# Modulation vectors on VectorE during the first projection, pool sums on GpSimd: one layer block on one core

## What is computed

```python
mod_x = silu(c) @ w_mod + b_mod                  # [1024] @ [1024, 6144]
mod_c = silu(c_ctx) @ w_mod + b_mod
sh1, sc1, gt1, sh2, sc2, gt2 = split(mod_x, 6)   # csh1, csc1 from mod_c

h_x = rmsnorm(x, g_pre_mix) * (1 + sc1) + sh1    # h_c likewise from ctx
u, q, k, v = split(h_x @ w_in, 4)                # k and v also of h_c
attn = neighbourhood_attention(q, k, v, k_c, v_c, rpb)
pool = pool_mixer(u)       # 4 groups: windowed means of 2, 4, 8, 16 tokens minus u, @ pool_w
x = x + gt1 * rmsnorm(concat(pool, attn) @ w_out, g_post_mix)
h = rmsnorm(x, g_pre_mlp) * (1 + sc2) + sh2
x = x + gt2 * rmsnorm(square(relu(h @ w_mlp_in)) @ w_mlp_out, g_post_mlp)
```

## Time and profile before

| | us |
|---|---|
| median of 3 runs | 858.69 |
| lowest, highest | 855.11, 858.84 |
| the profiled execution, its own time | 856.64 |
| its span in the trace | 854.8 |
| u, q (from the first whole blocks) | 36 to 57 |
| k and v, with products 16 to 23 | 57.2 to 109.6 |
| near attention, to the last product with V | 109.7 to 152.1 |

### The profile page before, as it was taken

How to read it: one execution, slowest core, us unless ns; L and a number is a source line. 1 busy time by engine, 2 the same in 40 slices (tenths; PEclk the granted TensorE clock), 3 DMA queues, 4 the chain that set the end, 5 groups by cost and what they waited for, 6 DMA issues and landing times.

```text
span 854.8 us, 12416 instructions
## 1 busy us (share of the span) xinstructions
PE 826.4 (97%) x4602; PEld 674.8 (79%) x4602; DVE 546.7 (64%) x956; ACT 462.3 (54%) x873; POOL 44.8 (5%) x55
## 2 busy tenths in 40 slices
PE   5899999989999999999999999999999999999996
PEld 2697855868888888878888888887666788888885
DVE  2363278668887767557666666587566576666653
ACT  4573256466546545556555555566766565555542
POOL 1010000000000000000000000049000000000000
PEclk9999999999999999999999999999999999999999
DMA  9975549517987765247666655185023376666501
GB/s 349 373 315 208 204 157 355 178 47 238 323 274 248 226 199 176 91 142 275 206 210 202 198 188 163 38 335 181 26 78 120 99 256 219 215 202 213 176 1 50
DMA packets 45099, 165.76 MB, mean 194 GB/s; under 512 B 4976, under 2 KB 5104, under 8 KB 44784
## 3 DMA queue, kind: packets, MB, share of 16 engines
q1 hardware_dynamic: 44752, 164.45, 56.6%
q10 hardware_dynamic: 288, 0.52, 0.2%
HBM read 163.91 MB, written 1.05 MB: 193 GB/s over the span
## 4 chain that ended last, share of the span: by engine, by line
PE 75%; issue 1%; DVE 1%; ACT 1%; POOLq 0%; POOL 0%; ACTq 0%; DVEq 0%
PE ps L1465 23%; PE ps L1467 12%; PE ps L1492 11%; PE ps L1494 11%; PE ps L1496 11%; PE ps L1701 1%; PE ps L1775 1%; PE ps L1726 1%; PE ps L1745 1%; PE ps L1703 0%; PE ps L1938 0%; DVE sc L1135 0%; PE ps L1485 0%; PE ps L1487 0%; PE ps L1486 0%
## 5 line engine op out<-in xcount | busy, mean ns | idle before, releaser
L944 DVE TENSOR_TENSOR lo<-raw,hi 128x1024 fp32r<-128x1024 f32 (+2 forms) x247 | 294.0, 1218 | 119.1 <-ACT hi L502 118.8
L1465 PE MATMUL ps<-T,hi 128*128 128x512 f32 x864 | 303.7, 392 | 0.0
L502 ACT ACTIVATE hi<-raw 128x1024 fp32r<-128x1024 f32 (+2 forms) x247 | 249.6, 1044 | 14.7 <-DMA raw<-in_w_in_k 6.1
L1467 PE MATMUL ps<-T,lo 128*128 128x256 f32 x864 | 243.7, 282 | 0.0
L1465 PEld LDWEIGHTS ps<-T,hi 128*128 128x128 f32 x864 | 162.2, 188 | 35.0
L1492 PE MATMUL ps<-hi,T 128*128 128x512 f32 (+2 forms) x504 | 169.9, 395 | 0.7 <-DVE T L1215 0.7
L1494 PE MATMUL ps<-lo,T 128*128 128x512 f32 (+2 forms) x504 | 167.0, 389 | 0.0
L1496 PE MATMUL ps<-hi,T 128*128 128x512 f32 (+2 forms) x504 | 166.8, 389 | 0.0
L1467 PEld LDWEIGHTS ps<-T,lo 128*128 128x128 f32 x864 | 163.4, 189 | 2.4
L1496 PEld LDWEIGHTS ps<-hi,T 128*128 128x128 f32 x504 | 94.6, 188 | 19.8
L1494 PEld LDWEIGHTS ps<-lo,T 128*128 128x128 f32 x504 | 94.7, 188 | 19.4
(11 more groups left out here) (212 smaller groups left out, 759.2 us busy)
## 6 DMA issues: line engine op xcount, KB each, us to landing
raw<-in_ffn_down SPq DMA_DIRECT2D x44, 512.0 KB, 3.6
raw<-in_w_mod_p SPq DMA_DIRECT2D x40, 512.0 KB, 6.0
raw<-in_ffn_gate SPq DMA_DIRECT2D x40, 512.0 KB, 4.4
raw<-in_ffn_up SPq DMA_DIRECT2D x40, 512.0 KB, 4.2
raw<-in_w_mlp_out SPq DMA_DIRECT2D x32, 512.0 KB, 4.5
raw<-in_w_mlp_in SPq DMA_DIRECT2D x28, 512.0 KB, 4.5
raw<-in_w_out SPq DMA_DIRECT2D x16, 512.0 KB, 5.2
raw<-in_w_in_q SPq DMA_DIRECT2D x8, 512.0 KB, 5.7
```

What stands on the lines that cost most here:

```text
L502: e.activation(HI[SLOT[h]][:, 0:w], raw[n % RAW][:, 0:w], ACT.Copy).then_inc(s_hi, 1)
L944: e.tensor_tensor(LO[SLOT[h]][:, 0:w], raw[n % RAW][:, 0:w], HI[SLOT[h]][:, 0:w], ALU.subtract).then_inc(s_lo, 1)
L1465: e.matmul(o, a[:, k * P:(k + 1) * P], X[:, k].rearrange("p s w -> p (s w)"), start=(k == 0), stop=(k == KT - 1), skip_group_check=True)
L1467: m = e.matmul(o[:, 0:L], b[:, k * P:(k + 1) * P], Xh[:, k, :], start=False, stop=(k == KT - 1), skip_group_check=True)
```

## The change

It rearranges how sh2, sc2 and gt1 are made, and what goes along with it:

- sh2 and sc2: their part of w_mod is stored turned (`w_mod_c`, 16 chunks of kind "T", 128 output columns each, all 1024 inputs along the row). The vector c is spread over all partitions by one more transfer (into `G2`, which is free until the MLP), ScalarE applies silu to it (128x1024), and VectorE takes a dot product per chunk, `tensor_tensor_reduce` with the sum going straight into a column of `sh2` or `sc2`.
- gt1: eight more chunks of `w_mod_r`, summed by VectorE into `acc` as gt2 is.
- The order of the stream puts all 24 chunks between w_in_k 0 and w_out 2. They are worked off in `split` of VectorE, in the order of the stream. TensorE's products 16 to 39, `mod_turned` and `mod_part` are gone.
- `window(g)` moves word for word from VectorE to GpSimd, behind the clearing of its buffer.
- ScalarE makes all four copies of V, and both turned tiles of each near-attention step.
- Chunks 0 to 2 of w_out are split before the near attention, 3, 4 and 5 in its iterations 1, 3 and 8. ScalarE splits w_in_k 1 to 3 between its copies of q.
- The transfer of the gt2 bias into `G2` is issued later (at chunk H[40]), after a wait on both additions of the sh2 and sc2 biases.

```diff
     s = []
     for j in range(4):
         s += u[j:j + 1] + c[4 * j:4 * j + 4]
-    s += q + k[0:2] + c[16:18] + k[2:3] + c[18:21] + k[3:4] + c[21:24] + v + c[24:30]
-    for j in range(4):
-        s += o[j:j + 1] + c[30 + 3 * j:33 + 3 * j]
-    s += o[4:]
+    s += q + k[0:1] + d[0:1] + k[1:2] + d[1:3] + k[2:3] + d[3:6] + k[3:4] + d[6:9] + v[0:1] + d[9:12] + v[1:2] + d[12:]
+    s += v[2:3] + m[0:3] + v[3:4] + o[0:1] + m[3:5] + o[1:2] + m[5:8] + o[2:]
...
+        W_OUT_SPLIT = {1: 3, 3: 4, 8: 5}
...
# SyncE
                 if n == CH_AT["w_in_q", 0]:
+                    e.dma_start(silr, row[5:6, :].partition_broadcast(P)).then_inc(s_row, 16)
# GpSimd, behind the memset of pw
+            for g in range(4):
+                window(g)
# ScalarE
+            e.wait_ge(s_row, 16)
+            e.activation(silr, silr, ACT.Silu).then_inc(s_silr, 1)
             for a in range(4):
                 h = CH["w_in_q", a]
+                if a:
+                    split(CH["w_in_k", a])
...
-            mod_part(0)
             split(CH["w_in_v", 3])
             load_table(ACT.Exp)
+            split(CH["w_out", 2])
...
-            for i in (0, 2):
+            for i in range(4):
                 e.activation(V[:, i, :], ps[i][:, :], ACT.Copy).then_inc(s_vv, 1)
...
-                        e.wait_ge(s_ntr, 2 * m + 1)
...
-                        e.activation(PT1[2 * m % 4], ps[2][:, :], ACT.Copy).then_inc(s_npa, 1)
-                    if n in (3, 7):
-                        mod_part(n // 3)
-                    if 3 <= n < 9:
-                        split(CH["w_out", n - 3])
+                        for hh in range(2):
+                            e.wait_ge(s_ntr, 2 * m + hh + 1)
+                            e.activation(PT1[(2 * m + hh) % 4], ps[2 + hh][:, :], ACT.Copy).then_inc(s_npt, 1)
+                    if n in W_OUT_SPLIT:
+                        split(CH["w_out", W_OUT_SPLIT[n]])
# VectorE, sum_mod
+                if name == "w_mod_c":
+                    at = (sh2, sc2)[j // 8][:, j % 8:j % 8 + 1]
+                    e.wait_ge(s_silr, 1)
+                    e.tensor_tensor_reduce(out=r, in0=r, in1=silr, scale=1.0, scalar=0.0, op0=ALU.mult, op1=ALU.add,
+                                           accum_out=at).then_inc(s_msum, 1)
+                    return
...
# VectorE, behind the splits of w_in_u
-            split(CH["w_in_k", 2])
-            for g in range(3):
-                window(g)
-            split(CH["w_in_k", 3])
-            window(3)
-            split(CH["w_in_v", 1])
-            mod_part(0)
-            split(CH["w_in_v", 3])
+            split(CH["w_out", 2])
+            for v, dst in enumerate((sh2, sc2)):
+                e.wait_ge(s_msum, 8 * v + 8)
+                e.tensor_tensor(dst, dst, col(("b_sh2", "b_sc2")[v]), ALU.add).then_inc(s_mcol, 1)
...
-            for i in (1, 3):
-                e.tensor_copy(V[:, i, :], ps[i][:, :]).then_inc(s_vv, 1)
...
-                        e.tensor_copy(PT1[(2 * m + 1) % 4], ps[3][:, :]).then_inc(s_npd, 1)
-                    if n in (3, 7):
-                        mod_part(n // 3)
-                    if 3 <= n < 9:
-                        split(CH["w_out", n - 3])
+                    if n in W_OUT_SPLIT:
+                        split(CH["w_out", W_OUT_SPLIT[n]])
# TensorE
                 wstat(CH["w_in_k", a], ROT[a], 2)
-                for n in range(*((16, 16), (16, 18), (18, 21), (21, 24))[a]):
-                    mod_product(n)
...
-                if j == 1:
-                    e.wait_ge(s_k, 2)
-                    e.wait_ge(s_const, 1)
-                    mod_turned(0, 4)
...
-                        mod_product(24 + 2 * n)
-                        mod_product(25 + 2 * n)
...
-                    if n == 5:
-                        mod_turned(1, 7)
```

More of the change, by code:

```diff
@@ L55, in stream_plan @@
 def stream_plan():
-    c = [("w_mod_p", j, 1024, "C") for j in range(40)]
+    c = [("w_mod_p", j, 1024, "C") for j in range(16)]
+    m = [("w_mod_r", j, 1024, "M") for j in range(16)]
+    d = [("w_mod_c", j, 1024, "T") for j in range(16)]
     u, q, k, v = ([("w_in_" + name, j, 1024, "H") for j in range(4)] for name in "uqkv")
@@ L428, in _, with window @@
             e.memset(big[:, 8960:8960 + 4 * UP], 0.0).then_inc(s_pwz, 1)
+            def window(g):
+                before, n = uT[:, g, :], (WIN[g - 1] if g else 0)
+                e.wait_ge(s_u, g + 1)
+                e.wait_ge(s_pwz, 1)
+                for s in range(g + 1):
+                    a0, a1 = (1, 0) if s == 0 else (1 << (s - 1), 1 << (s - 1))
+                    e0, e1 = (a0 if s == 0 else a0 + 1), UP - a1
+                    if s:
+                        e.wait_ge(s_win, n)
+                    e.tensor_tensor(pw[s][:, e0:e1], before[:, e0 - a0:e1 - a0], before[:, e0 + a1:e1 + a1],
+                                    ALU.add).then_inc(s_win, 1)
+                    before, n = pw[s], n + 1
+                e.wait_ge(s_win, n)
+                e.wait_ge(s_inv, 16)
+                e.tensor_tensor(dT[:, g, :], before[:, 8:8 + L], inv[:, g, :], ALU.mult).then_inc(s_win, 1)
+                e.wait_ge(s_win, n + 1)
+                e.tensor_tensor(dT[:, g, :], dT[:, g, :], uT[:, g, 8:8 + L], ALU.subtract).then_inc(s_win, 1)
+            for g in range(4):
+                window(g)
             def scales(b):
@@ L1528, in quarter_turned @@
                                  stop=True)
-                m.then_inc(s_rowT, 1)
-            def mod_turned(v, bank):
-                e.wait_ge(s_rowA, v + 5)
-                e.wait_ge(s_rowD, v + 1)
-                for j in range(KT):
-                    m = e.matmul(ps[bank][:, j:j + 1], acc[:, j * P:(j + 1) * P], ones[:, 0:1], start=True, stop=True)
                 m.then_inc(s_rowT, 1)
```

143 lines of the change are left out of this document (40 added, 103 removed).

## The result

The changed kernel takes 854.72 us (median of 20 runs, 852.23 to 858.05) where the kernel before takes 860.07 on the same chip (20 runs): a ratio of 0.994 (0.9922 to 0.9957), or 5.3 us less. The forecast was 847.5, with 853.5 as its upper end. So the change is a gain, of about half the size forecast. The interval stays clear of no change, but 0.6% is little above the 0.5% that I had named as the least that such a measurement tells.

The account below looks back on a forecast made before the run. TensorE (97% busy) was taken to bound the kernel, VectorE too in the near attention. Gains of 4.8 us up to the first score and 5.0 in the near attention, 9.8 off 856.64, gave 846.8; 847.5 was taken, range 843 to 853.5.

Parts of the forecast that it names:

- the stretch of the sums: From the low half of w_in_k 0 to VectorE's first score operation: forecast 50.7 us, before 55.5.
- the port: SBUF interface GpSimd shares with VectorE: 18 window operations to cost VectorE 0.25 us each, 4.5 us in all.
- the broadcast of c: One more 512 KB transfer ahead of q's weights, said to be hidden and cost nothing.
- The near attention: First score operation to last product with V: forecast gain 5.0 us.
- plain step: Near-attention step without a split of a w_out chunk: TensorE to set it, at 3.5 us.
- Products off TensorE: k and v projections: three products and sixteen turning matmuls leave, together 5.5 us; v ends at about 104.1.
- The dot product: VectorE's 16 dot products of 128x1024 before the near attention: 1.20 us each, 19.2 us in all.
- The rival of two passes: Dot product on VectorE takes 2.3 us instead of 1.2, adding 17 us before the near attention: 864 us; chance 0.04.
- That rival: Windows on GpSimd starved by VectorE, pool matmuls wait, from 2.2 us an operation on: about 852 us; chance 0.04.
- As many weight chunks are transferred as before: Weight transfers cost nothing: VectorE frees a buffer in about 1.5 us, a chunk needs 1.3 us of transfer.
- The clock: Rival: gaps on TensorE in the near attention halve its clock; two falls 850 us, staying low 859; chance 0.09.
- VectorE late: Rival: port at 0.5 us or dot products at 1.3, first score at 109 to 111.5, 850 to 854 us; chance 0.19.

Follow-up runs that it names:

- a1_same: The changed kernel with nothing edited, profiled and timed again: 854.18 us, 0.9941 of the kernel before.
- b1: The changed kernel, with only 128 of 1024 columns transferred of each of the 24 chunks summed before the near attention: 852.15 us, 0.9928 of the kernel before.
- a2: The changed kernel without the 18 window operations on GpSimd, one memset in their place: 853.88 us, 0.9929 of the kernel before.
- b2: The changed kernel, all chunks transferred, but each of the 24 sums before the near attention on 128 of 1024 columns: 850.96 us, 0.9924 of the kernel before.
- b4: The changed kernel with the window sums moved back from GpSimd to VectorE: 853.42 us, 0.9941 of the kernel before.
- d1: The changed kernel with c2's five later sums and earlier w_out 3 split, both broadcasts in their first places: 850.11 us, 0.9887 of the kernel before.
- d3: The changed kernel with half of the near attention's copies of turned probabilities back on VectorE: 850.80 us, 0.9894 of the kernel before.
- d4: c2 with the broadcast of c back ahead of q's weights, the gates' broadcasts still behind w_out 7: 847.42 us, 0.9855 of the kernel before.
- a3: The changed kernel with the broadcast of c issued behind q's weights and its Silu later: 853.47 us, 0.9942 of the kernel before.
- b3: The changed kernel with c's broadcast behind q's weights and those of gate bias and gain behind w_out 7: 850.99 us, 0.9920 of the kernel before.
- c1: b3 with the last four of the gate's eight sums and their chunks moved behind the first score: 846.16 us, 0.9857 of the kernel before.
- c2: b3 with five gate sums moved into the near attention and the w_out 3 split ahead of it: 845.25 us, 0.9850 of the kernel before.
- c4: The kernel before with one unread 512 KB broadcast added ahead of q's weights: 861.97 us, 1.0026 of the kernel before.
- c3: b3 with 16 unread matmuls on TensorE ahead of the first score pair: 854.02 us, 0.9934 of the kernel before.
- e1: c2 with eight of the sixteen copies of turned probabilities back on VectorE: 849.47 us, 0.9893 of the kernel before.
- a4: The changed kernel with the broadcasts of gate bias and gain issued behind w_out 7: 853.49 us, 0.9929 of the kernel before.
- d2: The changed kernel with 128 of 1024 columns transferred and summed of each of the 24 chunks before the near attention: 848.30 us, 0.9866 of the kernel before.

## Why the prediction was wrong

The sum missed in three places. The first is what failed: the forecast span of 845 us became 852.4 in a1_same by 4.5 us in the stretch of the sums, where the port was priced too low and the transfers at nothing. Then come 1.9 us in the early stage, where the broadcast of c was priced at nothing, and 1.3 us in the rest, which go with a fall of the clock.

**The near attention: right in size, the plain steps for another reason.** Forecast 3.5 us for a plain step and 5.2 for one with a split, measured 3.36 and 5.07 to 5.27; 5.0 us of gain, measured 5.3. The plain steps were to be TensorE's, at 3.67 and a little less, with VectorE's own at 2.8. They are VectorE's, with 0.50 us of waiting for ScalarE's high half that the 2.8 left out; TensorE takes 3.70 a step (135.03 to 138.73 between score pairs in a1_same) and had gained a lead in the steps with a split. That both come to about the same was luck. In the steps with a split the chain was right. The timeline of VectorE in the first profile shows the chain that the prediction described, score operations at either end, which answer to the 4.79 us apart before:

```profile
128.31 0.58 DVE L1079 CUSTOM_DVE_ANT_1 sc<-ps,arena 128x416 f32<-128x416 f32 x1
...
132.24 1.22 DVE L973 TENSOR_TENSOR lo<-raw,hi 128x1024 fp32r<-128x1024 f32 x1 [1.27 <-ACT hi L527]
...
133.58 0.58 DVE L1079 CUSTOM_DVE_ANT_1 sc<-ps,arena 128x416 f32<-128x416 f32 x1
```

**Products off TensorE: right.** In a1_same its first score pair starts at 105.85, 48.4 us behind the low half of w_in_k 0 (forecast 104.1 less 55.5, 48.6), and it never waits for k or v weights.

**The dot product: right.** 1.22 us beside a still GpSimd, 1.20 forecast. The rival of two passes fell. GpSimd's operations took 1.60 us, with 1.72 forecast as the worst, and ended at 86 us (88 forecast), and TensorE didn't wait for them. That rival fell too.

**The port at 0.25 us an operation: the first step that failed, by its size.** I took 0.25 us for each of 18, since some would fall into VectorE's idle time. While they ran VectorE was idle for 0.78 us, and each cost 0.45: 8.1 us instead of 4.5. With the transfers taken away (b1) the stretch is still 53.6 us, 2.9 more than the forecast 50.7. My upper end of 0.5 was the right reading of the earlier trace rows, and the contention that the Trainium skill states ("GPSIMD Engine Reference", Key points) was borne out: by it I had named 9 us, and 8.1 were measured.

**"As many weight chunks are transferred as before", at no cost: the second step that failed.** This is true of the kernel and false of the stretch. The kernel before multiplied 8 of the 24 chunks while k ran and the other 16 between the scores of the near attention; the changed one needs all 24 ahead of the first score. 16 chunks of 0.52 MB are 8.4 MB; the windows above show 374 instead of 209 GB/s over 50 us, 8.25 MB more. I had looked at the share of the transfers from 80 to 100 us alone (0.77), and compared a chunk's 1.3 us of transfer with VectorE's 1.5 us, leaving out that 1.8 MB of relative bias and two broadcasts of 0.5 MB pass in the same stretch. With the port's cost away (a2) or VectorE's sums thinned (b2) the stretch is 52.3 us, 1.6 more than the forecast. So removing the port's cost alone gave 2.9 of its 8.1 us back. The two limits together make the 4.5 us that the stretch of the sums is longer than forecast (55.2 instead of 50.7): port 3.6 more than taken, waits for high halves 1.8 more (3.8 instead of 2), the other terms together 0.9 less.

**The broadcast of c: not hidden.** I said that it costs nothing because q's weights wait for ScalarE's order. In nine of the twelve profiles with it ahead of q, ScalarE waits 0.3 to 3.0 us for w_in_q 0; of the six with it behind q two have such a wait, of 0.7 and 0.8, and the kernel before has none. In a1_same:

```profile
42.22 1.06 ACT L527 ACTIVATE hi<-raw 128x1024 fp32r<-128x1024 f32 x1 [1.19 <-DMA raw<-in_w_in_q]
```

I leave out five profiles with a long half clock in the early stage (last section). Of the others the low half of w_in_k 0 stood at 56.2 to 58.7 in the eight with the broadcast ahead of q (a1, a2, b1, b2, b4, d1, d3, d4; mean 57.4), and at 55.4 to 56.9 in the four with it behind (a3, b3, c1, c2; mean 56.0). 1.4 us by this, 1.9 by c4's profile; the pair d4 and c2 showed 0.4 in the ratios.

**The point of departure.** The profiled execution of before took 856.64 us, and three runs had a median of 858.69. Beside the experiments its medians, of 9 to 25 runs each, were 858.1 to 860.1, so the execution that I had read was 1.5 to 3.4 us shorter than its median. Its granted clock over the span was 0.995; the execution-to-execution spread goes with this number (last section). The same sum from these medians would have been 848.3 to 850.3. This is why the spans of before and a1_same differ by 2.4 us and the medians by more.

**The clock.** Its rival had the fall right and its price wrong. TensorE stood for 7 us, the clock fell to 0.50, and the price within the near attention was nothing that c3 or c1, whose near attention began at 1.00 and took 35.7 us, could show. The half clock behind an idle gap that the Trainium skill describes ("TensorE: Matmul & The Clock Gate", HAM oscillation) did set in, once and not at every gap (1.75 us for the second score pair, 0.97 again from the third on); it was hidden here.

**The rivals.** "VectorE late" is the nearest to what happened: 0.45 us for each window, the first score a microsecond behind its 109 to 111.5 even in a1_same, but w_in_v 2 never late. Its time, 850 to 854, is the nearest. It had 0.19; it was ruled down because VectorE's idle time was to take up the windows, and because transfers were no part of it. The forecast's error was to treat VectorE as the one limit with the transfers and TensorE hidden behind it, when the three lay within 5 us of each other.

**The rest: one fall of the clock.** The rest of the span is 702.3 to 702.7 us in six profiles, 703.8 to 704.2 in eleven and 705.4 and 705.6 in two (e1, c4). They sort by the granted clock between the end of the near attention and 840 us. In the six, the kernel before's among them, it stays at 1.00. In the eleven it stands at 0.50 once, for some 3 us, in nine of them 33 us behind the near attention and in both profiles of the changed kernel in the second layer; in the two it does so twice. Windows of a1_same and b3_both_later:

```profile
612.70:616.00 3.30, 3.30 (x14) 2.48 (x11) 2.70 (x8) 1.53 (x7) 0.00 (x0) 0.50 0.00 0
```

```profile
177.10:180.40 3.30, 3.30 (x10) 2.56 (x9) 1.96 (x6) 2.60 (x7) 0.00 (x0) 0.50 0.00 0
```

So each such fall goes with about 1.5 us here, and the 1.3 us of the rest are one of them, not a cost of the new order of work. This sorts the profiles, and no run set the clock on its own. What stays open is why one execution has it and the next has not, and whether the change makes it more frequent.

## What to carry to other kernels

Before work is moved ahead of a point, count by the stretch and not by the kernel what must have landed by then: bytes over the measured rate is a limit like an engine's busy time, and next to a nearly full engine it decides how much of any relief comes through. When two limits lie within a few microseconds, thin each alone and then both; moving a part of the load behind the point relieved both at once here, and was worth more than the later broadcasts (by the ratios 4.6 us in d1, 1.8 in b3). Before two profiles are compared to a microsecond, count the stretches of half clock in each. An operation shifted to GpSimd beside a VectorE full of two-input instructions saves VectorE nothing if each costs it as much as it took there, as in b4.

## What the runs showed of the hardware

- Windows of 128x256 to 128x271 on GpSimd take 1.60 us beside VectorE's dot products (a1_same), and lengthen these from 1.22 to between 1.65 and 1.76 us. Such an operation takes 0.42 to 0.44 us on VectorE (b4).
- The 0.45 us that each operation of GpSimd cost VectorE is thus about the operation's own time on VectorE.
- Transfers held 401 GB/s over 50 us with a busy share of 1.02 (b2_thin_work).
- The time of an execution goes with its granted clock. Of the 25 executions of the kernel before beside the a kernels, the three with a mean clock of 0.997 took 855.9 to 857.0 us, and the four with 0.987 or 0.988 took 860.9 to 864.3.
- Executions of one kernel differ by up to 4 us by the low half of w_in_k 0 (61.05 and 57.45 for the changed kernel). In five profiles (the first one, a4, c3, d2, e1) it came at 58.6 to 61.1 us instead of 55.4 to 58.7; these five had the granted clock at 0.50 for over 8 us in a row before it. In d3, with two shorter stretches of it, the low half came at 57.5. Window of the first profile:

```profile
20.00:28.00 8.00, 8.00 (x52) 6.08 (x48) 2.12 (x7) 3.43 (x6) 0.00 (x0) 0.50 0.87 325
```

In the kernel before the clock fell there too, but for a shorter time (0.86 over 24 to 36 us). What makes it long in one execution and short in the next was not tried.
